# Gate/up weights of experts 4 to 31 in 4 MB transfers, and a new row order of the gathered tokens

## The chip, the cores and the metric

The program runs on one core of a Trainium2 chip. Its time is the device time of one execution in microseconds. The kernel before took 1258.95 us (median of three runs, 1258.73 to 1260.2). All weights and activations are float32 in HBM; the whole block is one launch.

## The reference, cut to what matters

One encoder layer on 256 tokens of width 1024. Three attention branches, gated and merged, are followed by a mixture of 32 experts, of which each token takes 4. The change touches the way in which the experts' weights come on chip, so this is the part to see:

```python
def moe_ffn(h, router_w, router_b, w_gu, b_gu, w_dn, b_dn):
    logits = (h @ router_w).astype(jnp.float32) + router_b.astype(jnp.float32)
    top_val, top_idx = lax.top_k(logits, TOP_K)          # 4 of 32
    top_w = jax.nn.softmax(top_val, axis=-1)
    ...
    def expert_block(args):
        xb, e = args
        gu = xb @ w_gu[e] + b_gu[e]                      # w_gu[e]: 1024 x 2048
        g = jnp.minimum(gu[:, :D_FF], SWIGLU_LIMIT)
        u = jnp.clip(gu[:, D_FF:], -SWIGLU_LIMIT, SWIGLU_LIMIT)
        a = (u + 1.0) * (g * jax.nn.sigmoid(SWIGLU_ALPHA * g))
        return a @ w_dn[e] + b_dn[e]                     # w_dn[e]: 1024 x 1024
```

Every expert's weights are read: 8 MB of gate/up and 4 MB of down for each of 32.

## The kernel before, in words

The program is written by hand for five engines, which wait for each other on semaphores. SP issues nearly all transfers, in the order of its program; a waiting SP holds back all that stands behind it.

A **ring** of 20 slots (8 KB of each of 128 partitions, 1 MB in all, per slot) lies in the tensor `arena`. While the attention part runs (`FRONT`, 42 chunks), six slots serve as its weight ring and the rest holds its work areas. Afterwards all 20 belong to the experts.

An expert is 12 **chunks** of 1 MB: eight of gate/up and four of down. They are streamed in pairs, so every transfer is 2 MB. `WEIGHT_PAIRS` is the order: gate/up of expert 0, then for n from 1 on gate/up of n followed by down of n-1, and down of expert 31 last. Chunk c goes into slot `(c + 12) % 20`. SP issues the pair that begins at c when `chunk_used` says that the two chunks that lay in its slots have been multiplied (line 446), and its landing raises the semaphore of the pair's first slot. The first eight chunks are issued from within the front (`EARLY_AFTER`).

A pair of gate/up is 256 rows of the matrix: partition p holds rows 2p and 2p+1 of them, which lie together, 16 KB. So a pair is one piece of 2 MB of HBM. A chunk is then one contraction step of 128 rows (every second one of the 256), and the tokens must be gathered in the same order. That is what `gather_half` does: it multiplies the normalised tokens `xn` by a selection matrix, with `xn` as the weight operand, and takes every second element of a row (a step of 8 bytes). The result, `XT`, is scaled by `g_cols`, whose order follows (`paired`, on the host). Down has four rows of 4 KB a partition, also 16 KB.

TensorE's order for expert n (n from 2 on) is: two bias products, gate/up steps k = 0 to 3, the scatter of expert n-2 and two transposes of weights, k = 4 and 5, half a gather for the next pair of experts, k = 6 and 7, down of expert n-1 (four chunks), four transposes of the activation (`turn_act`, which reads `sig` with a step of 16 bytes). Before each even k it waits for that pair's landing (`weights_landed`); the same holds for each pair of down. Two half gathers of 16 instructions (in the trace a float32 product is two) stand ahead of expert 0, and one in each of experts 0 to 29.

In the last expert, the scatter of expert 30 follows the landing of the last down pair (`close_second_last`), then down of 31, its scatter and the final norm.

All matrix instructions of these helpers carry line 497 in the trace (`mm`), and transposes their own lines (761 for the weights, 767 for the activation, 575 for tokens read without a step). Line 377 issues every expert transfer. An overflow loop for experts with more than 64 tokens follows; it is changed in the same way.

Of the kernel before, what the change touches and what calls it, by code (L numbers as in the profile page):

```python
# [25 lines left out]
P = 128  # L26
D = 1024
KC = D // P
# [11 lines left out]
EXPERTS, TOP_K = 32, 4  # L40
# [7 lines left out]
CHUNK = 2048  # L48
RING = 20
FRONT_RING = 6  # L50
# [5 lines left out]
EXPERT_CHUNKS = 12  # L56
# [12 lines left out]
NF = len(FRONT)  # L69
# [23 lines left out]
EARLY = 8  # L93
# [42 lines left out]
def down_chunk(n):  # L136
# [1 line left out]
    return gate_up_chunk(n + 1) + KC if n + 1 < EXPERTS else EXPERT_CHUNKS * EXPERTS - 4  # L138


WEIGHT_PAIRS = ([(0, j) for j in range(0, KC, 2)]
                + [pair for n in range(1, EXPERTS) for pair in [(n, j) for j in range(0, KC, 2)]
                   + [(n - 1, j) for j in range(KC, EXPERT_CHUNKS, 2)]]
                + [(EXPERTS - 1, j) for j in range(KC, EXPERT_CHUNKS, 2)])


def last_unit_of(o):
# [3 lines left out]
def build(nc, t):  # L151
# [1 line left out]
    w_mem = t["w_mem_kv"].rearrange("l (k p) c -> (l p) k c", p=P)  # L153
    w_out = t["w_out"].rearrange("l (k p) c -> (l p) k c", p=P)
    w_br = {b: t[f"w_{b}"].rearrange("l (k p) c -> (l p) k c", p=P) for b in ("branch_a", "branch_b", "branch_c")}
    w_gu = t["expert_w_gate_up"].rearrange("l e (k p a) c -> (l e) p k (a c)", p=P, a=2)
    w_dn = t["expert_w_down"].rearrange("l e (k p a) c -> (l e) p k (a c)", p=P, a=4)
    b_gu = t["expert_b_gate_up"]
    na_rows = t["na_rows"]
# [2 lines left out]
    with ExitStack() as ctx:  # L162
# [15 lines left out]
        xn = sb("x_normed", [P, T, D])  # L178
# [19 lines left out]
        ring = arena[:, 0:RING * CHUNK].rearrange("p (r c) -> p r c", r=RING)  # L198
# [74 lines left out]
        ps = ctx.enter_context(nc.psum_tensor("ps", [P, 8, 512], F32))  # L273
# [51 lines left out]
        def ring_slot(c):  # L325

            return (c + FRONT_SLOT) % RING

        def front_fills(r):

            return len(range(r, NF, FRONT_RING)) if r < FRONT_RING else 0

        def fills_through(c):

            return front_fills(ring_slot(c)) + c // RING + 1

        ALL_CHUNKS = EXPERTS * EXPERT_CHUNKS

        def overflow_fills(j):

            first = j // 2 * 2
            main = sum(ring_slot(c) == ring_slot(first) for c in range(0, ALL_CHUNKS, 2))
            return front_fills(ring_slot(first)) + main + 1

        def bcast(ap, axis, n):

# [20 lines left out]

        @block.sync
        def _(sp):
            def load_weights(e, j, r):  # L370

                assert j % 2 == 0 and r % 2 == 0
                if j < KC:
                    src = w_gu[bass.ds(e, 1), :, j // 2, :].rearrange("o p c -> (o p) c")
                else:
                    src = w_dn[bass.ds(e, 1), :, (j - KC) // 2, :].rearrange("o p c -> (o p) c")
                sp.dma_start(ring[:, r:r + 2, :].rearrange("p r c -> p (r c)"), src).then_inc(landed[r], 16)

            for tt in range(T):
                sp.dma_start(mem_raw[:, tt, :], t["mem"].rearrange("b (t p) d -> (b p) t d", p=P)[:, tt, :]).then_inc(mem_in[tt], 16)  # L380
# [2 lines left out]
            for i in range(NF):  # L383
                if i == 1:
                    sp.dma_start(x[:], t["x"].rearrange("b (t p) d -> (b p) t d", p=P)).then_inc(x_in, 16)
                    sp.dma_start(t5_in[0:T5_BUCKETS, :], t["t5_rel_bias"]).then_inc(t5_in_done, 16)
                    sp.dma_start(t5_in[T5_BUCKETS:T5_BUCKETS + 3, :], t["group_of_head"]).then_inc(t5_in_done, 16)
                    sp.dma_start(onehot[:], t["bucket_onehot"]).then_inc(t5_in_done, 16)
                if i >= FRONT_RING:
                    sp.wait_ge(chunk_used, i - FRONT_RING + 1)  # L390
                kind, n = FRONT[i]
                dst = ring[:, i % FRONT_RING, :]
                if i in WIDE_FIRST or i in WIDE_LAST:
                    late = int(i in WIDE_LAST)
                    first = (n - late) * SLOTS_W
                    src = {"mem": w_mem, "in": w_in}[kind][:, 4 * late:4 * late + 4, first:first + 2 * SLOTS_W]
                    dst = dst.rearrange("p (k c) -> p k c", k=4)
                elif kind in ("mem", "in", "out"):
                    src = {"mem": w_mem, "in": w_in, "out": w_out}[kind][:, :, n * SLOTS_W:(n + 1) * SLOTS_W]
                    dst = dst.rearrange("p (k c) -> p k c", k=KC)  # L400
                elif kind == "branch_b":
                    src, dst = w_br[kind], dst.rearrange("p (k c) -> p k c", k=2)
                else:
                    src, dst = w_br[kind][:, :, n * 512:(n + 1) * 512], dst.rearrange("p (k c) -> p k c", k=4)
                sp.dma_start(dst, src).then_inc(landed[i % FRONT_RING], 16)
                if i in EARLY_AFTER:
# [5 lines left out]
                    load_weights(*WEIGHT_PAIRS[c // 2], ring_slot(c))  # L412
                if i == T5_STORE_AFTER:
                    sp.wait_ge(t5_copied, 1)
                    sp.dma_start(t5_scratch, t5_rows).then_inc(t5_saved, 16)
                    sp.wait_ge(t5_saved, 16)
                for u in range(2, NU):
                    if i != IMAGE_AFTER[u]:
                        continue
                    if u - 2 >= IMAGES:  # L420
                        sp.wait_ge(scores_drained, u - IMAGES + 1)
                    row = image_rows(u)
                    rows, row = (na_rows, row) if row < NA_HEADS else (t5_scratch, row - NA_HEADS)

                    sp.dma_start(image[:, (u - 2) % IMAGES], bass.AP(rows.tensor, row * REL, [[1, P], [REL, 2], [1, IMG]])
                                 ).then_inc(image_in[(u - 2) % IMAGES], 16)
# [11 lines left out]
            sp.wait_ge(chunk_used, OUT0)  # L438
            load_bias()
            sp.dma_start(b_dn, t["expert_b_down"].rearrange("l e c -> (l e) c")).then_inc(b_dn_in, 16)  # L440
            for c in range(EARLY, ALL_CHUNKS, 2):
                r = ring_slot(c)
                if c >= RING:
                    sp.wait_ge(chunk_used, NF + c - RING + 2)
                elif r < FRONT_RING:
                    sp.wait_ge(chunk_used, max(i for i in range(NF) if i % FRONT_RING in (r, r + 1)) + 1)
                else:
                    sp.wait_ge(chunk_used, NF)
                load_weights(*WEIGHT_PAIRS[c // 2], r)
                if c == RING + 14:  # L450
                    sp.dma_start(final_g, bass.AP(t["final_norm_g"].tensor, 0, [[0, P], [1, D]])).then_inc(final_g_in, 16)
            sp.wait_ge(routed, 1)
            n_over = sp.value_load(ovf[0:1, MAX_OVERFLOW:MAX_OVERFLOW + 1], min_val=0, max_val=MAX_OVERFLOW)
            with sp.If(0 < n_over):
                sp.dma_start(far_iota, bass.AP(t["iota"].tensor, 0, [[0, P], [1, D]])).then_inc(iota_in, 16)
                with sp.Fori(0, MAX_OVERFLOW) as b:
                    with sp.If(b < n_over):
                        e_b = sp.value_load(ovf[0:1, bass.ds(b, 1)], min_val=0, max_val=EXPERTS - 1)

                        for j in range(0, EXPERT_CHUNKS, 2):  # L460

                            sp.wait_ge(chunk_used, b * EXPERT_CHUNKS + (NF + ALL_CHUNKS))
                            load_weights(e_b, j, ring_slot(j))
# [31 lines left out]
        def _(pe):  # L495
            def mm(out, lhsT, rhs, start, stop, **kw):
                return nc.tensor.matmul(out, lhsT, rhs, start=start, stop=stop, **kw)  # L497
# [199 lines left out]


            turn_x1(3)
            xn_pairs = xn[:].rearrange("p t (k q a) -> p t k q a", k=4, a=2)  # L700
            pe.wait_ge(consts_in, 96)
            for c in range(4):
                last = router_part(c)
# [21 lines left out]
            def gather_half(half, width, bank=3):  # L725

                for k in range(4):
                    for tt in range(T):
                        last = mm(ps[:, bank, k * P:k * P + width], xn_pairs[:, tt, 2 * half + k // 2, :, k % 2],
                                  P_pair[:, tt, 0:width], tt == 0, tt == T - 1)  # L730
                last.then_inc(gathered, 1)

# [80 lines left out]
            for n in range(EXPERTS):  # L813
# [51 lines left out]
            with pe.If(0 < n_over):  # L865
                with pe.Fori(0, MAX_OVERFLOW) as b:
                    with pe.If(b < n_over):
# [9 lines left out]
                        pe.wait_ge(gu_drained, n + 1)  # L877
                        bias_rows(1)
                        for k in range(KC):
                            if k % 2 == 0:  # L880
# [565 lines left out]
```

## Time and profile before

| | us |
|---|---|
| median of three runs | 1258.95 |
| the profiled execution | 1258.98 |
| its span, first to last instruction | 1257.1 |
| TensorE busy (modelled ends) | 1171.8 (93%) |
| VectorE, ScalarE, GpSimd busy | 279.1, 253.8, 221.0 |
| HBM read | 454.39 MB, 362 GB/s over the span |
| transfers of gate/up, of down | 128 and 64, each 2 MB |

The page cuts the span in 40 slices of 31.4 us. The attention part fills the first ten; the experts begin at about 330 us. From there on both the row of TensorE and that of the transfers stand at nine tenths and more, so the page alone does not say which of the two sets the end. The chain of waits and the stretches in the section of rows do.

### The profile page before, as it was taken

Reading aid. Unit: us, or ns where it says so; the run is one execution under the profiler, and the core shown is the slowest. Engines: PE = TensorE matmul, PEld = TensorE weight load, DVE = VectorE, ACT = ScalarE, POOL = GpSimd, SP = SyncE. Lnnn points to the kernel's source line nnn. Section 1 sums busy time; section 2 is a strip of 40 time slices with the busy share of each in tenths; the row PEclk is TensorE's granted clock in tenths of the full one; section 3 lists DMA queues with packets and bytes.
Section 4 is the critical chain, followed back from the end, with each engine's and each line's share of the span. In section 5 each row is a group of like instructions: output and inputs, shape, how many; then the busy total and the mean of one; then the engine's idle time right before and its main releaser. Section 6 shows DMA issues by size and latency. Waiting matters only on the chain.

```text
span 1257.1 us, 14083 instructions
## 1 busy us (share of the span) xinstructions
PE 1171.8 (93%) x6107; PEld 592.8 (47%) x6107; DVE 279.1 (22%) x520; ACT 253.8 (20%) x533; POOL 221.0 (18%) x96
## 2 busy tenths in 40 slices
PE   6999998998899999999999999899999999999986
PEld 6989776898433334333333333333333333333322
DVE  3147265231421111111111112111111111111111
ACT  6455455333211000101000101000100000000002
POOL 6866766685100000000000000000000000000000
PEclk9999999998999999999999999999999999999999
DMA  9755543594999999999999999999999999999994
GB/s 326 229 170 152 190 143 106 202 363 161 373 389 425 427 428 429 425 428 428 427 429 426 427 429 427 427 428 429 427 428 428 429 428 426 429 426 428 428 427 178
DMA packets 67174, 456.39 MB, mean 363 GB/s; under 512 B 4425, under 2 KB 32777, under 8 KB 42536
## 3 DMA queue, kind: packets, MB, share of 16 engines
q1 hardware_dynamic: 66904, 455.18, 88.6%
q8 instruction: 49, 0.80, 0.3%
q0 software_dynamic: 208, 0.30, 0.1%
q14 instruction: 13, 0.11, 0.0%
HBM read 454.39 MB, written 1.07 MB: 362 GB/s over the span
## 4 chain that ended last, share of the span: by engine, by line
PE 49%; DMA 39%; DVE 4%; ACT 3%; POOL 3%; issue 1%; SPq 0%; DVEq 0%; ACTq 0%; POOLq 0%
PE ps L497 47%; DMA arena<-in_expert_w_gate_up 31%; DMA arena<-in_expert_w_down 7%; POOL w_parts L484 3%; ACT arena L954 2%; DMA arena<-in_w_mem_kv 1%; DVE row_max L1228 1%; DVE neg_max L1235 1%; DVE arena L1218 1%; DVE arena L1225 1%; PE ps L767 1%; ACT w_parts L934 1%; PE ps L761 1%; PE ps L542 0%; DVE b_tmp L1233 0%
## 5 line engine op out<-in xcount | busy, mean ns | idle before, releaser
L497 PE MATMUL ps<-arena,gathered_T 128*64 128x512 f32 x2048 | 464.8, 598 | 27.1 <-DMA arena<-in_expert_w_gate_up 24.9
L497 PE MATMUL ps<-arena 128*64 128x512 f32 (+5 forms) x1482 | 328.3, 572 | 26.3 <-DMA arena<-in_expert_w_down 24.4
L497 PEld LDWEIGHTS ps<-arena,gathered_T 128*64 128x64 f32 x2048 | 138.7, 136 | 292.5 <-issue 240.1
L484 POOL TENSOR_TENSOR w_parts<-arena,w_parts 128x1024 fp32r<-128x1024 f32 x84 | 211.2, 2539 | 88.7 <-ACT w_parts L934 88.0
L497 PEld LDWEIGHTS ps<-arena 128*64 128x64 f32 (+3 forms) x1482 | 114.0, 149 | 229.3 <-issue 185.4
L497 PE MATMUL ps<-w_parts,h_T_parts 128*128 128x256 f32 (+1 forms) x576 | 102.1, 335 | 4.3 <-POOL w_parts L484 4.3
L934 ACT CAST w_parts<-arena 128x1024 fp32r<-128x1024 f32 x82 | 81.8, 1046 | 104.5 <-PE ps L497 102.1
L497 PEld LDWEIGHTS ps<-w_parts,h_T_parts 128*128 128x128 f32 x576 | 86.2, 190 | 19.4 <-POOL w_parts L484 5.6
L1338 DVE TENSOR_SCALAR arena<-arena 128x128 f32<-128x128 f32 x64 | 19.3, 343 | 294.2 <-PE ps L761 294.2
L1344 DVE TENSOR_SCALAR arena<-ps 128x512 f32<-128x512 f32 x32 | 22.1, 692 | 275.2 <-PE ps L497 275.2
L1069 ACT COPY arena<-ps 128x256 f32<-128x256 f32 x32 | 11.9, 373 | 347.7 <-PE ps L761 347.7
L497 PEld LDWEIGHTS ps<-arena,x_normed 128*128 128x128 f32 x512 | 62.7, 196 | 25.8 <-issue 24.3
L497 PE MATMUL ps<-h_T_parts,w_parts 128*128 128x256 f32 x576 | 70.4, 283 | 1.7 <-POOL w_parts L484 1.3
L1060 ACT ACTIVATE gathered_T<-ps,g_cols 128x128 f32<-128x128 f32 x128 | 36.6, 369 | 174.3 <-PE ps L497 174.3
L497 PEld LDWEIGHTS ps<-h_T_parts,w_parts 128*128 128x128 f32 x576 | 69.0, 189 | 3.2 <-POOL w_parts L484 1.5
L497 PE MATMUL ps<-arena,x_normed 128*128 128x128 f32 x512 | 68.6, 288 | 1.2 <-DVE arena L1299 1.2
L1353 DVE COPY arena<-ps 128x512 f32<-128x512 f32 x32 | 22.1, 692 | 187.8 <-PE ps L767 187.8
L1077 ACT COPY arena<-ps 128x512 f32<-128x512 f32 x32 | 18.8, 586 | 203.7 <-PE ps L497 203.7
L1073 ACT ACTIVATE arena<-arena 128x512 f32<-128x512 f32 x32 | 20.2, 630 | 109.7 <-DVE arena L1344 109.7
L497 PE MATMUL ps<-w_parts,merged_T_parts 128*128 128x256 f32 x192 | 26.9, 302 | 3.7 <-ACT merged_T_parts L920 3.0
L767 PEld LDWEIGHTS ps<-ident,arena 128*128 128x128 f32 x128 | 17.9, 209 | 25.9 <-issue 25.9
L954 ACT ACTIVATE arena<-arena,neg_max 128x256 f32<-128x256 f32 x48 | 23.8, 497 | 28.7 <-DVE neg_max L1235 28.7
(165 smaller groups left out, 569.5 us busy)
## 6 DMA issues: line engine op xcount, KB each, us to landing
arena<-in_expert_w_gate_up SPq DMA_DIRECT2D x128, 2048.0 KB, 43.5
arena<-in_expert_w_down SPq DMA_DIRECT2D x64, 2048.0 KB, 45.1
arena<-in_w_in SPq DMA_DIRECT2D x29, 1024.0 KB, 5.4
arena<-in_w_mem_kv SPq DMA_DIRECT2D x4, 1024.0 KB, 13.0
arena<-in_w_out SPq DMA_DIRECT2D x4, 1024.0 KB, 7.4
arena<-t_scratch SPq DMA_DIRECT2D x6, 384.0 KB, 3.9
arena<-in_w_branch_a SPq DMA_DIRECT2D x2, 1024.0 KB, 5.0
arena<-in_w_branch_c SPq DMA_DIRECT2D x2, 1024.0 KB, 5.1
```

Source lines behind the costliest of these rows:

```text
L484: last = nc.gpsimd.tensor_tensor(wHL[:, i % 2, 1, half], ring[:, i % FRONT_RING, half], wHL[:, i % 2, 0, half].bitcast(F32), ALU.subtract)
L497: return nc.tensor.matmul(out, lhsT, rhs, start=start, stop=stop, **kw)
L761: last = nc.tensor.transpose(ps[:, 3, tt * P:(tt + 1) * P], PW[:, tt, :], ident[:])
L767: last = nc.tensor.transpose(ps[:, 2, f * P:(f + 1) * P], sig.rearrange("p (q f) -> p f q", f=4)[:, f, :], ident[:])
L934: nc.scalar.copy(wHL[:, i % 2, 0, half], ring[:, i % FRONT_RING, half]).then_inc(high_ready, 1)
L954: last = nc.scalar.activation(p, p, ACT.Exp, bias=neg_max[:, o, 2 * hh + tt:2 * hh + tt + 1], accum_out=exp_sum[:, u, 2 * hh + tt:2 * hh + ...
L1060: last = nc.scalar.mul(xt[:, c, 0:width], ps[:, bank, k * P:k * P + width], g_cols[:, 3 * KC + c:3 * KC + c + 1])
L1073: nc.scalar.activation(sig, gate_c, ACT.Sigmoid, scale=ALPHA).then_inc(sig_ready, 1)
L1077: nc.scalar.copy(y_sb, ps[:, bank, :]).then_inc(y_ready, 1)
L1338: last = vec.tensor_scalar(PW[:, tt, :].rearrange("p (a s) -> p a s", a=2), bcast(slots, 1, 2), key_tile[:, tt, e], w_sel[:, tt, e], ALU.i ...
L1344: vec.tensor_scalar(gate_c, ps[:, 0, :], LIMIT, None, ALU.min).then_inc(gate_ready, 1)
L1353: vec.tensor_copy(aT, ps[:, 2, :].rearrange("p (f s) -> p f s", f=4)).then_inc(aT_ready, 1)
```

## The change: what it does

Gate/up is laid out by rows of eight: partition p holds rows 8p to 8p+7 of an expert's matrix, which is 64 KB that lie together. Experts 0 to 3 still take it in four transfers of 2 MB, each 16 KB out of every 64. Experts 4 to 31 take it in two of 4 MB, each 32 KB out of every 64. Down is as before. The order of the chunks and their slots is the same; `TRANSFERS` maps the first chunk of each transfer to its expert, place and length m.

SP waits for m chunks to be used before it issues a transfer of m, and TensorE waits once for a transfer, which from expert 4 on is before k = 0 and k = 4. The tokens are gathered with a step of eight elements, 32 bytes, in place of two; the number of instructions is unchanged, and `g_cols` follows on the host.

```diff
-WEIGHT_PAIRS = ([(0, j) for j in range(0, KC, 2)] ...
+FIRST_LONG = 4
+
+def transfers():
+    short, long, down = [(j, 2) for j in range(0, KC, 2)], [(0, 4), (4, 4)], [(KC, 2), (KC + 2, 2)]
+    order = [(0, *t) for t in short]
+    for n in range(1, EXPERTS):
+        order += [(n, *t) for t in (short if n < FIRST_LONG else long)] + [(n - 1, *t) for t in down]
+    order += [(EXPERTS - 1, *t) for t in down]
...
-    w_gu = t["expert_w_gate_up"].rearrange("l e (k p a) c -> (l e) p k (a c)", p=P, a=2)
+    w_gu = t["expert_w_gate_up"].rearrange("l e (p a) c -> (l e) p (a c)", p=P)
...
-                    src = w_gu[bass.ds(e, 1), :, j // 2, :].rearrange("o p c -> (o p) c")
+                    src = w_gu[bass.ds(e, 1), :, j * CHUNK:(j + m) * CHUNK].rearrange("o p c -> (o p) c")
...
-                sp.dma_start(ring[:, r:r + 2, :].rearrange("p r c -> p (r c)"), src).then_inc(landed[r], 16)
+                sp.dma_start(ring[:, r:r + m, :].rearrange("p r c -> p (r c)"), src).then_inc(landed[r], 16)
...
-            for c in range(EARLY, ALL_CHUNKS, 2):
+            for c, (e, j, m) in TRANSFERS.items():
+                if c < EARLY:
+                    continue
...
-                    sp.wait_ge(chunk_used, NF + c - RING + 2)
+                    sp.wait_ge(chunk_used, NF + c - RING + m)
...
-            xn_pairs = xn[:].rearrange("p t (k q a) -> p t k q a", k=4, a=2)
+            xn_rows = xn[:].rearrange("p t (q a) -> p t q a", a=KC)
...
-                        last = mm(ps[:, bank, k * P:k * P + width], xn_pairs[:, tt, 2 * half + k // 2, :, k % 2],
+                        last = mm(ps[:, bank, k * P:k * P + width], xn_rows[:, tt, :, 4 * half + k],
...
-                    if k % 2 == 0:
+                    if c in TRANSFERS:
                         weights_landed(c)
...
-    paired = np.asarray(inputs["ffn_norm_g"]).reshape(KC // 2, P, 2).transpose(0, 2, 1).reshape(KC, P)
+    by_row = np.asarray(inputs["ffn_norm_g"]).reshape(P, KC).T
```

On SP, at the transfers of experts 3 and 4 (the transfer of `final_norm_g` stands in the middle of expert 3's). Before:

```order
L451 DMA x_tokens<-in_final_norm_g 128x1024
L377 DMA arena<-in_expert_w_gate_up 128x4096 x2
L377 DMA arena<-in_expert_w_down 128x4096 x2
L377 DMA arena<-in_expert_w_gate_up 128x4096 x4
L377 DMA arena<-in_expert_w_down 128x4096 x2
```

Now:

```order
L464 DMA x_tokens<-in_final_norm_g 128x1024
L388 DMA arena<-in_expert_w_gate_up 128x4096 x2
L388 DMA arena<-in_expert_w_down 128x4096 x2
L388 DMA arena<-in_expert_w_gate_up 128x8192 x2
L388 DMA arena<-in_expert_w_down 128x4096 x2
```

Up to expert 3 nothing moves; from expert 4 on two rows of 128 x 8192 stand where four of 128 x 4096 stood, each with one wait.

On TensorE, in expert 4: the bias products, gate/up, the scatter and the transposes (`landedN` is the semaphore of slot N). Before:

```order
L497 MATMUL ps<-bias_parts,pick 128x512 [waits pick_ready,gu_drained]
L497 MATMUL ps<-bias_parts,pick 128x512
L497 MATMUL ps<-arena,gathered_T 64x512 [waits landed16,XT_ready]
L497 MATMUL ps<-arena,gathered_T 64x512 x7
L497 MATMUL ps<-arena,gathered_T 64x512 [waits landed18]
L497 MATMUL ps<-arena,gathered_T 64x512 x7
L497 MATMUL ps<-arena 128x512 [waits y_ready]
L497 MATMUL ps<-arena 128x512 x3
L761 MATMUL ps<-ident,arena 128x128 [waits PW_ready]
L761 MATMUL ps<-ident,arena 128x128
```

Now:

```order
L509 MATMUL ps<-bias_parts,pick 128x512 [waits pick_ready,gu_drained]
L509 MATMUL ps<-bias_parts,pick 128x512
L509 MATMUL ps<-arena,gathered_T 64x512 [waits landed16,XT_ready]
L509 MATMUL ps<-arena,gathered_T 64x512 x15
L509 MATMUL ps<-arena 128x512 [waits y_ready]
L509 MATMUL ps<-arena 128x512 x3
L773 MATMUL ps<-ident,arena 128x128 [waits PW_ready]
L773 MATMUL ps<-ident,arena 128x128
```

The wait on slot 18 is gone and its sixteen products follow the wait on slot 16 directly, which now stands for both halves of the 4 MB. No instruction of TensorE changes its place.

## Rows read from the trace of the kernel before

**Rows 1.** The page's fourth part: the chain that ended last, by engine

```profile
PE 49%; DMA 39%; DVE 4%; ACT 3%; POOL 3%; issue 1%; SPq 0%; DVEq 0%; ACTq 0%; POOLq 0%
```

**Rows 2.** That chain in order of time: start us, us, what

```profile
629.79 9.27 PE ps L497 x48
639.08 40.29 DMA arena<-in_expert_w_gate_up
679.41 5.57 PE ps L497 x24
...
1195.15 45.16 DMA arena<-in_expert_w_down
1240.35 1.99 PE ps L497 x8
```

**Rows 3.** Stretches: length, each engine's busy us (instructions), clock, transfers' share, GB/s

```profile
366.00:370.00 4.00, 4.00 (x26) 2.45 (x24) 0.00 (x0) 0.21 (x1) 0.00 (x0) 1.00 0.72 221
374.00:376.00 2.00, 2.00 (x12) 0.72 (x10) 1.86 (x4) 0.63 (x1) 0.00 (x0) 1.00 0.90 246
...
400.00:640.00 240.00, 240.00 (x1158) 92.66 (x1156) 40.38 (x90) 24.80 (x64) 0.00 (x0) 1.00 1.01 427
640.00:1200.00 560.00, 515.77 (x2428) 193.24 (x2424) 85.54 (x191) 51.21 (x130) 0.00 (x0) 1.00 1.01 428
1200.00:1235.00 35.00, 29.71 (x134) 9.86 (x132) 3.99 (x8) 2.17 (x4) 0.00 (x0) 1.00 0.99 419
```

**Rows 4.** Transfers from 1000 to 1200 us: packets; issues with us to landing

```profile
DMA packets 5869, 85.48 MB, mean 427 GB/s; under 512 B 651, under 2 KB 651, under 8 KB 651
...
arena<-in_expert_w_gate_up SPq DMA_DIRECT2D x24, 2048.0 KB, 45.0
```

**Rows 5.** Transfers from 28 to 33 us (w_in, rows of 1 KB)

```profile
DMA packets 1703, 1.72 MB, mean 343 GB/s; under 512 B 27, under 2 KB 1703, under 8 KB 1703
```

**Rows 6.** Transfers from 60 to 75 us (w_in), GB/s in 40 slices

```profile
GB/s 371 382 382 388 238 87 27 0 0 0 0 0 0 0 0 68 82 224 350 380 393 385 382 390 142 0 0 0 0 0 0 0 0 0 25 87 117 300 366 380
```

**Rows 7.** Transfers from 260 to 265 us (w_out, rows of 1 KB)

```profile
DMA packets 1684, 1.71 MB, mean 343 GB/s; under 512 B 25, under 2 KB 1683, under 8 KB 1683
```

**Rows 8.** Weight loads of TensorE by form: busy us, mean ns | idle before

```profile
L497 PEld LDWEIGHTS ps<-arena,x_normed 128*128 128x128 f32 x512 | 62.7, 196 | 25.8 <-issue 24.3 <-DVE arena L1299 1.5
...
L767 PEld LDWEIGHTS ps<-ident,arena 128*128 128x128 f32 x128 | 17.9, 209 | 25.9 <-issue 25.9
...
L575 PEld LDWEIGHTS ps<-ident,x_tokens 128*128 128x128 f32 x16 | 1.8, 140 | 0.6 <-DVE x_tokens L1194 0.6
```

**Rows 9.** TensorE in order of time, the gathers up to 370 us

```profile
327.10 4.04 PE L497 MATMUL ps<-arena,x_normed 128*128 128x128 f32 x32 [1.22 <-DVE arena L1299]
...
343.63 2.15 PE L497 MATMUL ps<-arena,x_normed 128*128 128x128 f32 x16
...
367.60 2.15 PE L497 MATMUL ps<-arena,x_normed 128*128 128x128 f32 x16
```

**Rows 10.** Line 377 from 373 to 374 us: its one issue, and its landing

```profile
L377 SPq DMA_DIRECT2D arena<-in_expert_w_gate_up x1: 328/328/328, 373.4 to 373.4; - x1
...
DMA to landing us min/median/max: 8.1/8.1/8.1
```

**Rows 11.** Line 377 at 399.95 us, expert 4's second pair: issue, landing

```profile
L377 SPq DMA_DIRECT2D arena<-in_expert_w_gate_up x1: 328/328/328, 399.9 to 399.9; - x1
...
DMA to landing us min/median/max: 13.2/13.2/13.2
```

**Rows 12.** TensorE in order of time, expert 11's gate/up and scatter

```profile
620.41 7.09 PE L497 MATMUL ps<-arena,gathered_T 128*64 128x512 f32 x32
627.43 1.99 PE L497 MATMUL ps<-arena 64*128 64x512 f32 x8
```

**Rows 13.** TensorE in order of time, the end

```profile
1220.82 3.65 PE L497 MATMUL ps<-arena,gathered_T 128*64 128x512 f32 x16 [0.26 <-DMA arena<-in_expert_w_gate_up]
...
1230.60 3.65 PE L497 MATMUL ps<-arena 128*64 128x512 f32 x16 [1.15 <-DMA arena<-in_expert_w_down]
1234.19 0.75 PE L767 MATMUL ps<-ident,arena 128*128 128x128 f32 x4
1235.77 3.65 PE L497 MATMUL ps<-arena 128*64 128x512 f32 x16 [0.83 <-DVE arena L1353]
1240.35 1.99 PE L497 MATMUL ps<-arena 64*128 64x512 f32 x8 [0.93 <-DMA arena<-in_expert_w_down]
```

More of the change, by code:

```diff
@@ L138, in down_chunk @@
     return gate_up_chunk(n + 1) + KC if n + 1 < EXPERTS else EXPERT_CHUNKS * EXPERTS - 4
[L141 to L144, printed above, removed]
+FIRST_LONG = 4
[5 more added lines that the diff above has]
+    order += [(EXPERTS - 1, *t) for t in down]
+    c, out = 0, {}
+    for e, j, m in order:
+        out[c] = (e, j, m)
+        c += m
+    return out
+TRANSFERS = transfers()
 def last_unit_of(o):
@@ L333, in fills_through @@
         def fills_through(c):
-            return front_fills(ring_slot(c)) + c // RING + 1
+            return front_fills(ring_slot(c)) + sum(ring_slot(b) == ring_slot(c) for b in TRANSFERS if b <= c)
         ALL_CHUNKS = EXPERTS * EXPERT_CHUNKS
         def overflow_fills(j):
-            first = j // 2 * 2
-            main = sum(ring_slot(c) == ring_slot(first) for c in range(0, ALL_CHUNKS, 2))
-            return front_fills(ring_slot(first)) + main + 1
+            return front_fills(ring_slot(j)) + sum(ring_slot(c) == ring_slot(j) for c in TRANSFERS) + 1
         def bcast(ap, axis, n):
@@ L369, in _, with load_weights @@
         def _(sp):
-            def load_weights(e, j, r):
-                assert j % 2 == 0 and r % 2 == 0
+            def load_weights(e, j, m, r):
                 if j < KC:
-                    src = w_gu[bass.ds(e, 1), :, j // 2, :].rearrange("o p c -> (o p) c")
+                    src = w_gu[bass.ds(e, 1), :, j * CHUNK:(j + m) * CHUNK].rearrange("o p c -> (o p) c")
                 else:
                     src = w_dn[bass.ds(e, 1), :, (j - KC) // 2, :].rearrange("o p c -> (o p) c")
-                sp.dma_start(ring[:, r:r + 2, :].rearrange("p r c -> p (r c)"), src).then_inc(landed[r], 16)
+                sp.dma_start(ring[:, r:r + m, :].rearrange("p r c -> p (r c)"), src).then_inc(landed[r], 16)
             for tt in range(T):
@@ L411, in _ @@
                     c = EARLY_AFTER[i]
-                    load_weights(*WEIGHT_PAIRS[c // 2], ring_slot(c))
+                    load_weights(*TRANSFERS[c], ring_slot(c))
                 if i == T5_STORE_AFTER:
@@ L440, in _ @@
             sp.dma_start(b_dn, t["expert_b_down"].rearrange("l e c -> (l e) c")).then_inc(b_dn_in, 16)
-            for c in range(EARLY, ALL_CHUNKS, 2):
+            for c, (e, j, m) in TRANSFERS.items():
+                if c < EARLY:
+                    continue
                 r = ring_slot(c)
                 if c >= RING:
-                    sp.wait_ge(chunk_used, NF + c - RING + 2)
-                elif r < FRONT_RING:
-                    sp.wait_ge(chunk_used, max(i for i in range(NF) if i % FRONT_RING in (r, r + 1)) + 1)
+                    sp.wait_ge(chunk_used, NF + c - RING + m)
+                elif r + m <= FRONT_RING:
+                    sp.wait_ge(chunk_used, max(i for i in range(NF) if i % FRONT_RING in range(r, r + m)) + 1)
                 else:
                     sp.wait_ge(chunk_used, NF)
-                load_weights(*WEIGHT_PAIRS[c // 2], r)
+                load_weights(e, j, m, r)
                 if c == RING + 14:
@@ L458, in _ @@
                         e_b = sp.value_load(ovf[0:1, bass.ds(b, 1)], min_val=0, max_val=EXPERTS - 1)
-                        for j in range(0, EXPERT_CHUNKS, 2):
-                            sp.wait_ge(chunk_used, b * EXPERT_CHUNKS + (NF + ALL_CHUNKS))
-                            load_weights(e_b, j, ring_slot(j))
+                        sp.wait_ge(chunk_used, b * EXPERT_CHUNKS + (NF + ALL_CHUNKS))
+                        for j, m in ((0, 4), (4, 4), (KC, 2), (KC + 2, 2)):
+                            load_weights(e_b, j, m, ring_slot(j))
             for tt in range(T):
@@ L879, in _ @@
                         for k in range(KC):
-                            if k % 2 == 0:
+                            if k % 4 == 0:
                                 pe.wait_ge(landed[ring_slot(k)], (b + overflow_fills(k)) * 16)
@@ L1428 @@
     arrays.update(constants())
-    paired = np.asarray(inputs["ffn_norm_g"]).reshape(KC // 2, P, 2).transpose(0, 2, 1).reshape(KC, P)
+    by_row = np.asarray(inputs["ffn_norm_g"]).reshape(P, KC).T
     arrays["g_rows"] = np.concatenate([np.asarray(inputs[n]).reshape(KC, P)
-                                       for n in ("mem_norm_g", "attn_norm_g", "ffn_norm_g")] + [paired], 0)
+                                       for n in ("mem_norm_g", "attn_norm_g", "ffn_norm_g")] + [by_row], 0)
     rpb = np.asarray(inputs["na_rpb"])[0]
```

## The prediction

> **What bounds the kernel now.** I read the chain that ended last first. By engine it is half TensorE and two fifths transfers [rows 1], which alone decides nothing. In order of time it is plainer [rows 2]: TensorE's products form an unbroken chain until 639.08 us, and from there pieces of 40 to 45 us under transfers of expert weights alternate with a few us of products, up to the last down transfer, whose landing lets TensorE start at 1240.35. The reader should not take the first part as proof that TensorE bounds the kernel until 639 us: the chain goes back through the slot that a transfer waited for.
>
> The stretches settle it [rows 3]. From 400 to 640 us TensorE is busy throughout, yet the transfers' share is full too (1.01) and they move 427 GB/s; from 640 to 1200 us TensorE has 44 us of idle time in 560, and the rate is the same 428. So the stream of weights runs without a gap from 400 us to the end and never faster; TensorE was at first behind on what had landed, and catches up at 640. The end is the start of this stream, plus its bytes at 428 GB/s, plus what TensorE does after the last landing. The stream has gaps ahead of 400 us only: share 0.72 from 366 to 370 us and 0.90 from 374 to 376 [rows 3]. There SP waits for TensorE to free slots; the transfer issued at 373.4 us lands 8.1 us later [rows 10], of which 4.9 are its own 2 MB at 428 GB/s (an expert's 12 MB take 29.4). Whatever delays TensorE ahead of that moment delays the whole stream.
>
> So three things can move the time: the rate, TensorE's work ahead of 373 us, and a new hole or a later tail.
>
> **The rate.** From 1000 to 1200 us 5869 packets carried 85.48 MB, 651 of them under 512 B [rows 4]: one small closing packet for eight of 16 KB, per engine and transfer. What a packet costs beside its bytes I take from rows with small packets. With several transfers queued, 1 KB packets ran at 343 GB/s [rows 5], which is 47.8 ns a packet on each of 16 engines; 16 KB at 427 GB/s [rows 4] is 613.9 ns. A straight line through both leaves 47.8 - 1024 x (613.9 - 47.8)/15360 = 10.1 ns for the packet itself. In the short bursts between 60 and 75 us the full slices stand at about 388 GB/s [rows 6], 42.2 ns, and the same line leaves 4.1 ns. No row shows packets of 32 KB; I take the middle of both, 7.1 ns, because the stream is queued like the first and steady like the second.
>
> A transfer of 4 MB replaces two of 2 MB. If a row of 32 KB is one packet, each engine sends eight in place of sixteen, and one closing packet in place of two: 9 x 7.1 = 64 ns less. There are 28 experts with two such transfers, 56 in all: 3.6 us off the end, 2.1 and 5.1 us with the two ends of the line. If rows are still cut at 16 KB, only the closing packet goes: 56 x 7.1 = 0.4 us.
>
> Against it stands the new spacing in HBM. Before, a transfer was one piece of 2 MB; now each partition's piece begins 64 KB after the last. In the rows, weights read as 1 KB out of every 29 KB (w_in) and 1 KB out of every 4 KB (w_out) both run at 343 GB/s [rows 5, 7], so spacing by a power of two costs nothing that they show; I price it at zero and keep the loss as a rival. The Trainium skill, "DMA: Bandwidth & Descriptors", section on latency and other measured facts, says that copies of 16 KB rows lose speed when rows are large powers of two apart: 207 against 214 GB/s at 512 KB. It gives nothing for 64 KB; by its 3%, as an estimate, the long transfers would take 19 us more and the kernel about 1275. Rows 5 and 7 disagree with it at 4 KB, and no row here has 64.
>
> **The gathers.** Their instructions stay 16 per half, but the weight operand is read with a step of 32 bytes, not 8. The loads of the gathers take 196 ns; the only loads with a wider step, 16 bytes (line 767), take 209, and those of contiguous tokens (line 575) 140 [rows 8]. The last two are the same operation, so a step can add 69 ns to a load; but loads lie beside the product before, so most of that may not show. I take 209 - 196 = 13 ns for each of the 16, 0.2 us for a half gather, with 0 and 16 x 69 ns = 1.1 us as ends. Ahead of 373.4 us stand four halves: two at 327.10, one each at 343.63 and 367.60 [rows 9]. All are in TensorE's unbroken work there, so the stream starts 4 x 0.2 = 0.8 us later (0 to 4.4). Later halves are covered: TensorE has 44 us of idle time in some 19 experts of 29.4 us after 640 us [rows 3], 2.3 us each, and before it has landed chunks in hand. The Trainium skill, "SBUF — State Buffer", section on the DMA port swizzle, says that reads pay for each new 16-byte line, which a step of 16 and one of 32 bytes do alike; by it the price stays at 0.8 us. If the cost grew with the step it would be twice that, 1.7 us.
>
> **The longer waits.** SP now waits for four chunks, so the first half of a 4 MB transfer is issued when the second pair was. For expert 4 that is 399.95 us; that pair landed 13.2 us later, at 413.1 [rows 11]. On an idle queue 2 MB took 8.1 us [rows 10], so 4 MB issued there land no later than 399.95 + 8.1 + 4.9 = 412.95. No hole, with 0.2 us to spare, and the stream itself is 0.8 us late by then. Later the transfers are issued 45 us before they land [rows 4] and a pair's delay is about 6. What stands behind the waiting SP is only the next transfer. I price it at 0, up to 0.5 us.
>
> TensorE starts k = 0 when 4 MB have landed, 9.8 us apart. Thirty-two instructions take 7.1 us, the scatter and transposes 2.3 [rows 12]: it is done when the second half lands. In the last expert the second half lands where the last pair did, 1220.82 [rows 13]. From there: gate/up 7.0; down of 30, two runs of 3.6 (1230.60 to 1234.19); transposes and copy 1.6 (to 1235.77); the first half of down 31, 3.6. That ends at 1240.2, and the last landing releases TensorE at 1240.35. The tail stays as it is, with 0.15 us to spare; if the sum is off, it costs a few tenths.
>
> **Sum.** -3.6 + 0.8 = -2.8 us. The profiled execution took 1258.98 us around a span of 1257.1, which is the median of the runs shown (1258.95) to 0.03. Forecast: 1256.2 us. With the ends: 1258.98 - 5.1 = 1253.9, and 1258.98 - 2.1 + 4.4 = 1261.3.
>
> **Rivals.** First, packets do not grow or the loss is per byte: then -0.4 + 0.8, 1259.4. For it speaks that the trace has no packet over 16 KB; against it that the rate fell to 343 GB/s with small ones, so something is paid per packet. Second, the gathers pay the full 69 ns: -3.6 + 4.4, 1259.8; the gathers' 196 ns, already close to the 209 of the wider step, speak against it. Third, slower than before: the 64 KB spacing makes the engines' reads meet in HBM. The 56 transfers are 235 MB, 549 us at 428 GB/s, so each 1% of rate costs 5.5 us, and it decides from 0.5% on, below 426. At the lowest rate of a full stretch, 419 GB/s [rows 3], it costs 11.8 us, which with the gathers is 1271.6. The equal rates of rows 5 and 7 speak against it; for it, that no row shows pieces 64 KB apart.
>
> **How the numbers follow.** Less than 0.2% (2.5 us) is what a measurement of this kernel cannot tell from no change; faster means below 1256.4, slower above 1261.5. The forecast's case has 0.62, of which the packet price puts 0.43 below 1256.4 and 0.19 within. The first rival has 0.15 (0.13 within, 0.02 slower), the gathers 0.10 (0.07 and 0.03), the spacing 0.13, all slower. Together: faster 0.43, same 0.39, slower 0.18. The range runs from 1253.8 to 1262: it holds the forecast's ends and the first two rivals, and leaves out most of the third. The likeliest case by itself spans 1253.9 to 1258.
>
> **What would show it.** In the profile after: fewer packets (from 400 us on about a third fewer of the large ones) and a rate of 429 to 430 GB/s from 640 to 1200 us. If packets are as many as before, the first rival holds; a rate below 426 is the third. Loads of the gathers above 220 ns, and an issue at 373.4 us that moves to 374.2 or beyond, give the gathers' price. A share below 1.00 between 400 and 415 us would be the hole that I deny, and an idle time of TensorE before 1240 us that is gone would be a longer tail. The forecast is wrong if the rate rises by over 1.5% or falls at all.

## The result, and the profile after

The changed kernel is slower: 1267.93 us (median of 4 runs, 1267.55 to 1269.56) against 1259.34 (4 runs, 1258.73 to 1260.2), a ratio of 1.0068 with an interval of 1.0056 to 1.0080. The forecast was 1256.2 us, with a range up to 1262. The profiled execution took 1267.55 us around a span of 1265.7, which is 8.6 us more than before.

The stretches of the kernel after come first (from and to, length, busy us and instructions of PE, PEld, DVE, ACT and POOL, granted clock, transfers' share, GB/s):

```profile
326.00:334.00 8.00, 7.86 (x32) 7.67 (x32) 5.63 (x20) 1.24 (x5) 0.00 (x0) 0.79 1.01 430
334.00:344.00 10.00, 8.91 (x33) 2.79 (x34) 1.29 (x7) 1.04 (x4) 0.00 (x0) 0.83 0.49 184
369.00:373.00 4.00, 4.00 (x14) 1.92 (x14) 1.34 (x4) 0.37 (x1) 0.00 (x0) 0.57 0.99 426
374.00:376.00 2.00, 2.00 (x10) 0.82 (x7) 0.00 (x0) 0.00 (x0) 0.00 (x0) 1.00 0.00 0
411.00:414.00 3.00, 3.00 (x16) 1.01 (x14) 2.21 (x4) 0.63 (x1) 0.00 (x0) 1.00 0.62 180
640.00:1200.00 560.00, 558.77 (x2514) 237.88 (x2512) 87.47 (x196) 53.44 (x136) 0.00 (x0) 1.00 1.00 430
```

The first two of these stretches before:

```profile
326.00:334.00 8.00, 5.67 (x40) 4.47 (x42) 7.39 (x29) 2.29 (x8) 0.00 (x0) 1.00 1.00 430
334.00:344.00 10.00, 10.00 (x47) 3.31 (x44) 0.57 (x3) 0.00 (x0) 0.00 (x0) 1.00 1.00 416
```

In the last row of the kernel after, the stream is a little faster than in [rows 3], 430 against 428 GB/s, while TensorE's idle time fell from 44 us to 1.2 us. In the rows above it the stream has more gaps: from 374 to 376 us nothing moves at all (share 0.90 before), and from 411 to 414 us the share is 0.62, in a part that had been full. The granted clock, 1.00 before in all of these places, is 0.57 to 0.83 in three rows.

The transfers from 1000 to 1200 us, against [rows 4] (issues, then KB each and median us to landing):

```profile
DMA packets 3901, 85.88 MB, mean 429 GB/s; under 512 B 432, under 2 KB 432, under 8 KB 432
...
arena<-in_expert_w_gate_up SPq DMA_DIRECT2D x14, 4096.0 KB, 36.4
```

A third fewer packets for the same bytes: a row of 32 KB is one packet, and rival one is out. The weight loads by form, against [rows 8] (busy us, mean ns, idle before):

```profile
L509 PEld LDWEIGHTS ps<-arena,x_normed 128*128 128x128 f32 x512 | 124.1, 334 | 25.8 <-issue 24.3 <-DVE arena L1311 1.5
L779 PEld LDWEIGHTS ps<-ident,arena 128*128 128x128 f32 x128 | 18.1, 210 | 25.9 <-issue 25.9
L587 PEld LDWEIGHTS ps<-ident,x_tokens 128*128 128x128 f32 x16 | 1.8, 140 | 0.6 <-DVE x_tokens L1206 0.6
```

The gathers' loads went from 196 to 334 ns; the transposes that the price was read from did not move. The gathers' products, before and after:

```profile
L497 PE MATMUL ps<-arena,x_normed 128*128 128x128 f32 x512 | 68.6, 288 | 1.2 <-DVE arena L1299 1.2
L509 PE MATMUL ps<-arena,x_normed 128*128 128x128 f32 x512 | 130.0, 409 | 1.2 <-DVE arena L1311 1.2
```

The first number behind a bar is busy time, in which instructions that overlap count once. It grew by 61.4 us for the loads (62.7 to 124.1) and by 61.4 for the products, 1.92 us for each of the 32 half gathers. The loads were busy in 62.7 of the products' 68.6 us even before, so there was little product time left to hide a longer load in.

What that does to TensorE stands in its instructions in order of time (start, us, instruction, count), against [rows 9]:

```profile
325.97 7.89 PE L509 MATMUL ps<-arena,x_normed 128*128 128x128 f32 x32 [1.22 <-DVE arena L1311]
335.09 8.78 PE L509 MATMUL ps<-arena,gathered_T 128*64 128x512 f32 x32 [1.23 <-ACT gathered_T L1072]
...
348.05 4.07 PE L509 MATMUL ps<-arena,x_normed 128*128 128x128 f32 x16
...
375.46 4.07 PE L509 MATMUL ps<-arena,x_normed 128*128 128x128 f32 x16
```

Two halves take 7.89 us where they took 4.04, and one takes 4.07 where it took 2.15: 1.92 us a half gather, all of it TensorE's time. The 32 products after the first gather take 8.78 us in place of 7.09, in a stretch with a granted clock of 0.83. SP's last two issues that a standing stream waits for, in place of those of [rows 10, 11] (each with its landing):

```profile
L388 SPq DMA_DIRECT2D arena<-in_expert_w_gate_up x1: 327/327/327, 383.2 to 383.2; - x1
...
DMA to landing us min/median/max: 7.3/7.3/7.3
...
L388 SPq DMA_DIRECT2D arena<-in_expert_w_gate_up x1: 328/328/328, 411.6 to 411.6; - x1
...
DMA to landing us min/median/max: 12.1/12.1/12.1
```

The issue of 373.4 us now comes at 383.2, and expert 4's first 4 MB are issued at 411.6 and land at 423.7. The last view is the chain in order of time, the last of its longest pieces (start, us, what), against [rows 2]:

```profile
1112.64 18.06 PE ps L509 x80
1130.72 39.00 DMA arena<-in_expert_w_gate_up
1169.76 11.27 PE ps L509 x48
1181.05 37.89 DMA arena<-in_expert_w_gate_up
1218.98 10.70 PE ps L509 x40
1230.05 13.88 PE ps L509 x64
```

Before, the chain turned into transfers at 639; now it is products until 1130. The page's fourth part reads "PE 83%; DMA 6%", against [rows 1]. That does not make TensorE the bound: the stream is full from 640 to 1200 us, and TensorE, whose work for an expert grew from 26.6 to 28.5 us (one half gather each), still needs less than the 29.3 us of the expert's 12 MB. It only takes until 1130 to catch up.

How late each point of the stream is, by the two traces:

| point | before, us | after, us | late, us |
|---|---|---|---|
| the issue of [rows 10] | 373.4 | 383.2 | 9.8 |
| its landing | 381.5 | 390.5 | 9.0 |
| landing of expert 4's first 4 MB | 413.1 | 423.7 | 10.6 |
| last landing | 1240.3 | 1248.4 | 8.1 |
| end of the span | 1257.1 | 1265.7 | 8.6 |

The first 9.8 us are TensorE's: four half gathers cost 3.85 + 1.92 + 1.92 = 7.7 us, two stretches at the lower of the clock's two levels (335 and 369 us) cost 1.7 + 1.5 = 3.2, and the first gather began 1.1 us earlier. The landing takes 0.8 us of this back, the hole at expert 4 adds 1.6, another 2.5 come back over the rest of the stream (what the rate gains, less some smaller gaps), and the tail gives up 0.5.

### The profile page after: what moved, and what is told of

The parts are those of the page before. It is cut to its first block, busy times and chain, and to the rows that moved or that the text cites. A ratio compares the mean times of both kernels' runs of the same rounds, so it can differ in the third digit from the quotient of the medians.

```text
span 1265.7 us, 14027 instructions
## 1 busy us (share of the span) xinstructions
PE 1226.2 (97%) x6107; PEld 657.2 (52%) x6107; DVE 279.4 (22%) x520; ACT 253.6 (20%) x533; POOL 221.0 (17%) x96
## 4 chain that ended last, share of the span: by engine, by line
PE 83%; DMA 6%; DVE 4%; ACT 3%; POOL 2%; issue 1%; DVEq 0%; SPq 0%; ACTq 0%; POOLq 0%
PE ps L509 79%; DMA arena<-in_expert_w_gate_up 6%; POOL w_parts L496 2%; ACT arena L966 2%; PE ps L779 2%; PE ps L773 1%; DVE row_max L1240 1%; DVE neg_max L1247 1%; DVE arena L1230 1%; DVE arena L1237 1%; ACT w_parts L946 0%; PE ps L554 0%; PE ps L516 0%; DVE b_tmp L1245 0%; DMA arena<-in_mem 0%
## 5 line engine op out<-in xcount | busy, mean ns | idle before, releaser
L509 PE MATMUL ps<-arena 128*64 128x512 f32 (+5 forms) x1482 | 323.4, 571 | 1.8 <-ACT arena L1089 0.9
L509 PEld LDWEIGHTS ps<-arena,x_normed 128*128 128x128 f32 x512 | 124.1, 334 | 25.8 <-issue 24.3
L509 PE MATMUL ps<-arena,x_normed 128*128 128x128 f32 x512 | 130.0, 409 | 1.2 <-DVE arena L1311 1.2
L509 PE MATMUL ps<-w_parts,merged_T_parts 128*128 128x256 f32 x192 | 26.6, 299 | 3.7 <-ACT merged_T_parts L932 3.0
```

## Experiments

Theory G: the price of the new step of 32 bytes, paid by the half gathers ahead of the stream's last gap, delays the stream; the long transfers themselves gain about 3 us. Rivals: the 64 KB spacing or the long transfers' longer waits cost the time, or the gathers cost it in all experts and not only ahead of 383 us. A run is compared with runs of the kernel before on the same chip, by the ratio of the two; their medians were 1259.6 to 1260.0 us.

**Short transfers, new layout** (the step and the spacing stay, the long transfers go):

```
-FIRST_LONG = 4
+FIRST_LONG = EXPERTS
```

> The changed kernel with FIRST_LONG = 32: the new row order and the 32-byte step, but 2 MB transfers throughout. G: the late start of 8 to 10 us stays, the hole of 2 us and the gain of rate go: 1268 to 1271 us. H: no wait for four chunks is left, so the loss goes: 1259 to 1261 us. If the 64 KB spacing alone lowers the rate, it stands below 427 GB/s between 640 and 1200 us.

Measured: 1269.61 us, 1.0071 [1.0056, 1.0086], as G says. The long transfers are not what costs the time. The issue of [rows 10] comes at 384.3. The stretch of the steady stream:

```profile
640.00:1200.00 560.00, 560.00 (x2520) 237.98 (x2518) 87.92 (x196) 53.44 (x136) 0.00 (x0) 1.00 1.01 428
```

The rate is that of [rows 3] with every piece of 16 KB standing 64 KB after the last: the spacing, rival three of the prediction, costs nothing. The clock falls here too, in this row:

```profile
369.00:373.00 4.00, 4.00 (x13) 1.74 (x14) 1.34 (x4) 0.37 (x1) 0.00 (x0) 0.50 0.85 365
```

**Before, with the first four half gathers done twice** (narrow step, 2 MB; the second pass writes the same values):

```
-for k in range(4):
+for k in [k for _ in range(times) for k in range(4)]:   # times = 2 for the four halves ahead of 373 us, else 1
```

> The kernel before with the first four half gathers done twice (the two ahead of expert 0, and those of experts 0 and 1): 4 x 2.1 us more of TensorE's work ahead of the issue at 373 us. G: the stream of weights starts 8 to 9 us later and the kernel takes 8 to 9 us more, 1267.5 to 1269. Rival (TensorE's idle time after 640 us absorbs it): within 1 us of before.

Measured: 1266.82 us, 1.0062 [1.0046, 1.0077], 7.8 us by the ratio and a little under what was expected. Its issue, in place of that of [rows 10], its clock in the stretch just shown, and its stretch of [rows 3]:

```profile
L377 SPq DMA_DIRECT2D arena<-in_expert_w_gate_up x1: 328/328/328, 381.1 to 381.1; - x1
```

```profile
369.00:373.00 4.00, 4.00 (x22) 1.70 (x22) 1.33 (x4) 0.37 (x1) 0.00 (x0) 1.00 0.95 406
640.00:1200.00 560.00, 517.60 (x2444) 195.09 (x2442) 83.72 (x188) 51.84 (x133) 0.00 (x0) 1.00 1.01 428
```

The doubling adds 3.77 + 1.89 + 1.89 = 7.6 us of TensorE's time, with neither the new layout nor long transfers; the issue moves by 7.7 us and the end of the span by 7.5. The gathers take as long here as in the kernel after (7.81 us for the first two halves), but the clock stays at 1.00: this is the cost of the gathers without that of the clock.

**Before, with the other 28 half gathers done twice** (the same edit, `times = 2` from the third expert's gather on).

> The kernel before with the other 28 half gathers done twice: 28 x 2.1 = 59 us more of TensorE's work, all after the stream of weights has started. G: covered, within 1.5 us of before. Rival (the gathers cost wherever they stand): tens of us more.

Measured: 1260.51 us, 1.0009 [1.0000, 1.0018]:

```profile
640.00:1200.00 560.00, 558.40 (x2818) 236.44 (x2814) 87.09 (x195) 52.84 (x135) 0.00 (x0) 1.00 1.01 427
```

TensorE has as little idle time left as in the kernel after. The added half gathers took 53 us, not the 59 that were expected (1.9 us each), and cost 1.1 us by the ratio, 2.3 at the upper end of the interval: the later halves are covered, all but a little. The rival that charges the gathers in all experts falls.

**Long transfers from expert 8 on:** `FIRST_LONG = 8`.

> The changed kernel with FIRST_LONG = 8: the 32-byte step stays, the 4 MB transfers begin four experts later. G: by then the queue is deeper, the hole of 2 us near 411 us goes, 0.5 us of the rate's gain too: 1266 to 1267. H (waiting for four chunks makes a hole wherever it begins): the hole moves to expert 8 and the time stays at 1268.

Measured: 1267.82 us, 1.0052 [1.0036, 1.0067], against 1.0068 for the changed kernel. The intervals overlap and the medians are alike (1267.82 and 1267.93), so that a later start gains time is not shown here. The place of the hole, where the row of the kernel after had a share of 0.62:

```profile
411.00:414.00 3.00, 3.00 (x16) 1.00 (x14) 1.29 (x2) 0.63 (x1) 0.00 (x0) 1.00 1.02 431
```

The share is full there, and no gap shows at expert 8. In the changed kernel the first long transfer was issued 0.2 us before the last landing of what was queued ahead of it.

**A step of 16 bytes** (blocks of 512 rows, each partition holding four neighbours; 4 MB in one piece):

```
-w_gu = ....rearrange("l e (p a) c -> (l e) p (a c)", p=P)
+w_gu = ....rearrange("l e (h p a) c -> (l e) p h (a c)", p=P, a=4)
...
-xn_rows[:, tt, :, 4 * half + k]
+xn_rows[:, tt, half, :, k]
...
```

> The changed kernel with gate/up laid out by blocks of 512 rows (partition p holds four rows, 32 KB, and a 4 MB transfer is one piece of HBM); the gather's step is 16 bytes. If every step of a line or more costs alike, its loads stay at 334 ns, the stream starts 8 to 10 us late and the time is 1266 to 1268. If loads cost as the transposes of line 767 at the same step (209 ns), half a gather takes 2.2 to 2.4 us, the stream starts at most 1 us late, and with the faster rate the time is 1256 to 1258.

Measured: 1268.57 us, 1.0068 [1.0054, 1.0082], the first case but for half a microsecond.

```profile
L509 PEld LDWEIGHTS ps<-arena,x_normed 128*128 128x128 f32 x512 | 121.8, 328 | 25.8 <-issue 24.3 <-DVE arena L1311 1.5
```

The load costs at 16 bytes what it costs at 32 (328 and 334 ns), where 8 bytes cost 196: a step up between 8 and 16 bytes, not a slope. This agrees with the Trainium skill, "SBUF — State Buffer", section "Door 1: The DMA port swizzle", by which each new 16-byte line is paid for; the forecast cited it for equal prices, which holds, and took the price itself from another operation. A 4 MB transfer is one piece of HBM here, and from 640 to 1200 us the stream moves 430 GB/s, as with the pieces 64 KB apart.

**The changed kernel with contiguous gathers** (GpSimd writes the normalized tokens in the gathers' order):

```
-last = nc.gpsimd.tensor_scalar(xn[:, tt, :], x[:, tt, :], rstd[:, 2, tt:tt + 1], None, ALU.mult)
+last = nc.gpsimd.tensor_scalar(xn[:, tt, :].rearrange("p (a q) -> p q a", a=KC),
+            x[:, tt, :].rearrange("p (q a) -> p q a", a=KC), rstd[:, 2, tt:tt + 1], None, ALU.mult)
...
-xn_rows[:, tt, :, 4 * half + k]
+xn[:, tt, (4 * half + k) * P:(4 * half + k + 1) * P]
```

> The changed kernel, but GpSimd writes the normalised tokens in the gather's order, so the gather reads its weight operand without a step; the 4 MB transfers stay. Theory G (the 32-byte step of the gathers starts the stream of weights later): a half gather falls from 4.0 us to 2.1 or less, the issue at 383.2 us moves back to about 374, and with the faster rate the time is 1255 to 1257 us. Rival H (the longer wait for four chunks, the hole at expert 4, is the loss): the hole of 2 us stays and the time is 1264 to 1268 us.

Measured: 1260.43 us, 0.9997 [0.9988, 1.0006]. The loss is gone, and the gain has not come. GpSimd's write here, and that of the kernel before (busy us, mean ns):

```profile
L502 POOL TENSOR_SCALAR x_normed<-x_tokens,rstd 128x1024 f32<-128x1024 f32 x2 | 7.4, 3738 | 9.4 <-DVE rstd L1278 9.4
```

```profile
L490 POOL TENSOR_SCALAR x_normed<-x_tokens,rstd 128x1024 f32<-128x1024 f32 x2 | 5.7, 2838 | 9.4 <-DVE rstd L1265 9.4
```

and the stretch and the products of the first gather:

```profile
326.00:334.00 8.00, 6.26 (x33) 5.90 (x32) 7.28 (x29) 1.33 (x5) 0.00 (x0) 0.60 1.01 432
```

```profile
327.69 6.09 PE L510 MATMUL ps<-arena,x_normed 128*128 128x128 f32 x32 [1.52 <-DVE arena L1312]
```

The scattered write takes 0.9 us more each, and the gather, whose loads are down to 198 ns, falls into a stretch at the lower clock: 6.09 us for 4.04. The expectation missed both.

**Before, with the same GpSimd write** (2 MB transfers, the gathers contiguous).

> The kernel before with the tokens written in the gather's order (gather without a step, transfers unchanged). G: a step of 8 bytes cost little, so half a gather stays within 0.3 us of 2.15 and the time within 1.5 us of before, 1258 to 1260.5; if GpSimd's strided write is slow, its 5.7 us grow and the time with them. H says nothing else: 1259.

Measured: 1262.53 us, 1.0016 [1.0008, 1.0025], above what was expected; the write takes 3767 ns here. Both start the stream alike (this issue at 377.8 us, the last kernel's at 377.5), so their difference, 2.1 us of medians and 2.7 of spans, is what the long transfers gain in all, their longer waits and tail included.

**The changed kernel with the ordered write on ScalarE**, after the router's exponentials, and none on GpSimd:

```
...
+    last = nc.scalar.mul(xn[:, tt, :].rearrange("p (a q) -> p q a", a=KC),
+                         x[:, tt, :].rearrange("p (q a) -> p q a", a=KC), rstd[:, 2, tt:tt + 1])
...
```

> The changed kernel, with the tokens written in the gather's order as in e1_contig_gather, but by ScalarE after the router's exponentials, so that GpSimd's slower strided write (3.7 us against 2.8 each) no longer holds the first gather. G: TensorE keeps its full clock through the first gathers, the last issue that the stream waits for stands at 373 to 374.5 us, no hole at expert 4, and the faster rate is left over: 1255.5 to 1257.5. If the strided write is no faster there, or the clock falls anyway, 1259 to 1261.

Measured: 1255.76 us, 0.9971 [0.9960, 0.9981], 0.3% under the kernel before, and so under both. Its loads, its first gather and the clock of that stretch:

```profile
L505 PEld LDWEIGHTS ps<-arena,x_normed 128*128 128x128 f32 x512 | 59.5, 191 | 25.8 <-issue 24.3 <-DVE arena L1312 1.5
```

```profile
326.82 3.84 PE L505 MATMUL ps<-arena,x_normed 128*128 128x128 f32 x32 [1.22 <-DVE arena L1312]
```

```profile
326.00:334.00 8.00, 5.95 (x42) 4.42 (x44) 7.39 (x30) 2.81 (x9) 0.00 (x0) 1.00 1.00 426
399.00:411.00 12.00, 12.00 (x60) 4.26 (x58) 3.37 (x5) 1.22 (x2) 0.00 (x0) 1.00 0.97 397
```

The issue of [rows 10] stands at 372.7 us, 0.7 earlier than before. At expert 4 the first 4 MB still land 11.3 us after the landing before them (397 GB/s in that stretch), against 9.7 in the steady stream. That this is the hole of the changed kernel is not shown: it was issued 3.6 us ahead of the queue's last landing, the kernel with GpSimd's ordered write issued it 3.7 us ahead and shows 9.6, and a later 4 MB of this kernel on a deep queue took 11.2 as well (landing at 590.8 us). In the last expert TensorE waits 4.4 us for the whole 4 MB and then runs at the lower clock:

```profile
1207.29 8.52 PE L505 MATMUL ps<-arena,gathered_T 128*64 128x512 f32 x32 [4.40 <-DMA arena<-in_expert_w_gate_up]
```

**The same, long transfers for experts 6 to 30 only:**

```
-FIRST_LONG = 4
+FIRST_LONG = 6
...
-        order += [(n, *t) for t in (short if n < FIRST_LONG else long)] + [(n - 1, *t) for t in down]
+        order += [(n, *t) for t in (long if FIRST_LONG <= n < EXPERTS - 1 else short)] + [(n - 1, *t) for t in down]
```

> e8_contig_act with 4 MB transfers for experts 6 to 30 alone. The hole of 1.6 us that e8 still has at its first 4 MB transfer (11.3 us between two landings, where 9.7 is its own length) should go, since the queue is deeper by expert 6, and the last expert's wait for 4 MB (its gate/up ran at half clock after 4.4 us of idle) too: 2 us less from the first, 0.5 from the second, 0.4 us of the rate's gain lost: 1253 to 1255. If the queue's depth has no part in it, the time stays at 1255.8.

Measured: 1254.31 us, 0.9967 [0.9954, 0.9979]:

```profile
400.00:411.00 11.00, 11.00 (x54) 3.90 (x52) 2.51 (x4) 1.08 (x2) 0.00 (x0) 1.00 1.01 429
```

```profile
1235.76 1.99 PE L505 MATMUL ps<-arena 64*128 64x512 f32 x8 [0.92 <-DMA arena<-in_expert_w_down]
```

No gap shows at expert 4 or at expert 6, and the last landing releases TensorE again, as in [rows 13]. The interval overlaps that of the last kernel, so that this is the better of the two is not shown; that it is 0.3% under the kernel before, and under the changed one, is.

**Before, with ScalarE's ordered write** (2 MB transfers), to see whether the write alone gains.

> The kernel before with the tokens written in the gather's order by ScalarE, as in e8_contig_act, and its 2 MB transfers kept. If e8's gain comes from the long transfers, this one stays within 1 us of before (the start 0.5 us earlier, as half a gather takes 2.05 us): 1258.5 to 1259.5. If it comes from the quicker gathers and the freed GpSimd, it reaches 1256.

Measured: 1259.80 us, 1.0001 [0.9992, 1.0010]. The contiguous gathers alone gain nothing that shows; the 0.3% of the last two kernels comes with the long transfers.

## Why the prediction was wrong

**The bound was right.** "Whatever delays TensorE ahead of that moment delays the whole stream": 7.6 us put there in the kernel before cost 7.8 by the ratio, and 53 us put behind it cost 1.1.

**The gathers are the step that failed.** It said "I take 209 - 196 = 13 ns for each of the 16, 0.2 us for a half gather, with 0 and 16 x 69 ns = 1.1 us as ends." Measured were 138 ns a load and 1.92 us a half, above the upper end: 7.7 us ahead of the stream in place of 0.8 (0 to 4.4). The 209 ns belong to transposes, whose loads pay 69 ns for a step of 16 bytes over contiguous ones; a gather's load pays 137 at 16 bytes and 143 at 32 over its contiguous 191, twice as much. The price was carried from one operation to another by comparing the wrong pair: 196 and 209 ns differ in operation and in step at once. Nor was it right that "loads lie beside the product before, so most of that may not show": the loads were busy in 62.7 of the products' 68.6 us in the kernel before, and what they grew by shows in the products to the full. The forecast's own sign, "Loads of the gathers above 220 ns", came out.

**The hole was denied and came, at 2.1 us.** The 4 MB took 11.85 us from the landing before them to their own, against 9.7 in the steady stream. The bound in the prediction held the issue at 399.95 us; it came at 411.6. The 9.8 us by which TensorE was late account for most of that, and expert 2's half gather, which lies between the two issues, for the other 1.9: it is the gathers' price once more. The landing before it came at 411.9, so the queue was all but empty, and the 12.1 us to the landing are what a lone 2 MB (7.3) and 2 MB more (4.9) take. Not all of the hole is the long transfer's: with long transfers from expert 8 on, or none, the first 2 MB of expert 4 landed 5.9 and 6.1 us after the landing before them, against 4.9.

**The clock was not in the sum.** No row of before showed it below 1.00 there, so the 3.2 us were left out. Where they fall varies: the short-transfer kernel has nothing of it after its first gather (32 products in 7.09 us) and all of its 3.2 us from 366 to 376. The four traced kernels with a step of 16 or 32 bytes all lose time to the clock near 370 us, with 1.5 to 3.3 us in all, and the kernel before with its first halves doubled, whose gathers take as long, loses none. The step is not the only way to it, as both kernels with GpSimd's ordered write fall to 0.60 and 0.58 from 326 to 334 us. Why the clock falls in the one and not in the other stays open.

**The rate was right.** Packets of 32 KB exist, and the rate rose to 430 GB/s as forecast. In the middle of the stream, from the last landing of expert 7 to that of expert 29, 22 experts took 650.6 us before and 647.1 after (650.5 to 650.8 in the five other kernels with 2 MB there, 646.9 to 647.4 in the five others with 4 MB). That is 3.5 us for 44 long transfers, so 4.4 for all 56: above the 3.6 forecast and inside its ends of 2.1 and 5.1. Gaps between landings took part of it again, which left 2.5 us to the last landing here and 3.2 between the two kernels with GpSimd's ordered write. The spacing costs nothing, as priced: 428 GB/s with 2 MB. The loss that the Trainium skill, "DMA: Bandwidth & Descriptors", section on latency and other measured facts, gives for rows 512 KB apart, against which the prediction weighed this price, does not show at 64 KB.

**The tail** gave 0.5 us: TensorE sat idle for 4.4 us before the last expert's first 4 MB landed, then ran 32 products in 8.78 us in place of 7.09 (granted clock 0.76 from 1219 to 1226 us). The prediction had 0.15 us to spare.

```profile
1218.98 8.78 PE L509 MATMUL ps<-arena,gathered_T 128*64 128x512 f32 x32 [4.38 <-DMA arena<-in_expert_w_gate_up]
```

Put right, the sum goes 7.7 + 3.2 - 1.1 = 9.8 us to the issue of [rows 10], -0.8 to its landing (7.3 us in place of 8.1), +1.6 to expert 4's first 4 MB (the hole's 2.1, less 0.5 by which the kernel before had the larger gaps on the same way), -2.5 to the last landing and +0.5 to the end: 8.6 us, which is what the spans differ by. The 1.1 us by which the first gather began earlier lie ahead of all that the change touches; in the other traces it began between 2.9 us earlier and 1.4 later than before.

## What to carry to other kernels

A layout chosen for longer transfers sets the step of whatever reads the same index on chip; price that read from rows of the same operation, and where none shows the wider step, hold the price for unknown and let the range reach beyond another operation's difference. Look at busy time beside the mean: an operation whose loads fill its time already can hide no longer load. Find the last gap of the bounding stream: TensorE's time ahead of it counts in full, and behind it 53 us cost 1.1 here. Start long transfers once the queue is deep, and keep short ones at the end, where the wait for a whole transfer shows; the traces speak for both, the times do not yet tell them apart.

## What the runs showed of the hardware

- A weight load of the gathers' float32 products of 128 x 128 takes 191 ns with contiguous columns (197 and 198 where the clock was lower in the first gather), 196 at a step of 8 bytes, 328 at 16 and 334 at 32. For the transposes it is 140 contiguous and 209 at 16.
- With the step of 32 bytes two half gathers take 7.89 us where the granted clock was 0.79 and 7.87 where it was 1.00 (short transfers), both from 326 to 334 us; contiguous ones take 6.09 us at 0.60 and 3.84 at 1.00.
- GpSimd takes 3738 ns for 128 x 1024 float32 when each element is written 512 bytes after the last in runs of 8, 2838 when contiguous; ScalarE wrote the same order in 2024 ns.
- Rows of 32 KB travel as one packet: 3901 packets in place of 5869 for the same bytes, and 430 GB/s in place of 428.
- Between executions with near-identical work the granted clock fell to its lower level or stayed: in the changed kernel 0.79 from 326 to 334 us, in the short-transfer kernel 1.00, both with the same gather behind an idle time of 1.22 us. What sets it there stays open.
